# The relative bias of a second attention: from reversing products on TensorE to keys kept in reverse order

## The reference

```
rel = (kj[None, :] - pad_len) - qi[:, None]
bias = rel_bias[:, jnp.clip(rel, -REL_CLIP, REL_CLIP) + REL_CLIP]      # (8 heads, 257 numbers each)
s = jnp.einsum('bhqd,bhkd->bhqk', q_blk, kb).astype(jnp.float32) + bias
valid = (start - pad_len + kj) >= 0
p = jax.nn.softmax(jnp.where(valid, s, -jnp.inf), axis=-1)
return jnp.einsum('bhqk,bhkd->bhqd', p.astype(vb.dtype), vb)
```

## Time and profile before

| | us |
|---|---|
| median of 3 runs | 2052.92 (2052.65 to 2053.29) |
| the profiled execution: its own time | 2052.41 |
| the profiled execution: span | 2050.5 |
| PE busy | 1834.5 (89%) |
| DVE busy | 774.1 (38%) |
| ACT busy | 496.1 (24%) |
| POOL busy | 47.6 (2%) |

### The profile page before, as it was taken

One profiled execution on the slowest core, in us unless ns is written; L12 is line 12 of the kernel. 1 busy time (PEld: TensorE's weight loads), 2 busy tenths in 40 slices (PEclk: granted clock), 3 DMA queues, 4 the chain that ended last, 5 costly groups with the idle time before them and its releaser, 6 DMA issues. The chain is left out here.

```text
span 2050.5 us, 24148 instructions
## 1 busy us (share of the span) xinstructions
PE 1834.5 (89%) x9870; PEld 1133.4 (55%) x9871; DVE 774.1 (38%) x1035; ACT 496.1 (24%) x573; POOL 47.6 (2%) x74
## 2 busy tenths in 40 slices
PE   5989687999999988989898994898799989988998
PEld 5864464333333323333333231876699977568887
DVE  5535553112222112211221122548545466455444
ACT  3323411001010101010010001423334343334442
POOL 5000000000000000000000000100000000000000
PEclk9999898999999999999999997899899999989999
DMA  8549558999999999999999996534354544664551
GB/s 289 177 124 327 178 215 369 417 427 429 428 429 428 429 428 429 428 429 428 429 428 429 428 427 231 165 134 164 120 206 164 192 141 161 210 225 142 200 190 61
DMA packets 133235, 597.27 MB, mean 291 GB/s; under 512 B 16720, under 2 KB 16856, under 8 KB 108464
## 3 DMA queue, kind: packets, MB, share of 16 engines
q1 hardware_dynamic: 120096, 587.23, 72.4%
q10 hardware_dynamic: 12528, 7.50, 1.3%
q0 software_dynamic: 544, 1.59, 0.2%
HBM read 595.17 MB, written 1.11 MB: 291 GB/s over the span
## 5 line engine op out<-in xcount | busy, mean ns | idle before, releaser
L167 DVE TENSOR_TENSOR wl<-raw,wh 128x2048 fp32r<-128x2048 f32 x126 | 285.0, 2299 | 85.9 <-ACT wh L161 85.6
L161 ACT ACTIVATE wh<-raw 128x2048 fp32r<-128x2048 f32 x126 | 236.7, 1910 | 202.5 <-PE banks L195 120.2
L1200 PE MATMUL banks<-moe_halves,xs 128*64 128x512 f32 x1024 | 234.1, 605 | 12.0 <-DMA moe_halves<-in_w_exp_in 12.0
L211 PE MATMUL banks<-xth,wh 128*128 128x256 f32 x800 | 227.0, 284 | 7.0 <-DVE xtl L272 6.7
L211 PE MATMUL banks<-xtl,wh 128*128 128x256 f32 x800 | 225.8, 282 | 0.0
L211 PE MATMUL banks<-xth,wl 128*128 128x256 f32 x800 | 225.5, 282 | 0.0
L1249 DVE COPY hid<-banks 128x512 f32<-128x512 f32 x32 | 22.1, 691 | 521.5 <-PE banks L1200 521.5
L1200 PEld LDWEIGHTS banks<-moe_halves,xs 128*64 128x64 f32 x1024 | 71.0, 139 | 161.0 <-issue 128.8
L211 PEld LDWEIGHTS banks<-xth,wh 128*128 128x128 f32 x800 | 150.6, 188 | 8.1 <-DVE xtl L272 7.1
L211 PEld LDWEIGHTS banks<-xth,wl 128*128 128x128 f32 x800 | 152.0, 190 | 0.0
L211 PEld LDWEIGHTS banks<-xtl,wh 128*128 128x128 f32 x800 | 151.7, 190 | 0.3
(11 more groups left out here) (355 smaller groups left out, 2088.3 us busy)
## 6 DMA issues: line engine op xcount, KB each, us to landing
moe_halves<-in_w_exp_in SPq DMA_DIRECT2D x64, 2048.0 KB, 34.7
moe_left<-in_w_exp_in SPq DMA_DIRECT2D x34, 2048.0 KB, 33.5
moe_halves<-in_w_exp_out SPq DMA_DIRECT2D x32, 2048.0 KB, 31.1
raw<-in_mlp_w SPq DMA_DIRECT2D x64, 1024.0 KB, 5.7
raw<-in_w_exp_in SPq DMA_DIRECT2D x30, 2048.0 KB, 34.7
raw<-in_ada_w SPq DMA_DIRECT2D x48, 1024.0 KB, 5.8
raw<-in_w_exp_out SPq DMA_DIRECT2D x18, 2048.0 KB, 31.1
moe_left<-in_w_exp_out SPq DMA_DIRECT2D x14, 2048.0 KB, 33.9
```

What stands on the lines that cost most here:

```text
L161: act.activation(c.wh[:, slot], c.raw[:, slot], ACT.Copy).then_inc(c.high_ready, 1)
L167: dve.tensor_tensor(c.wl[:, slot], c.raw[:, slot], c.wh[:, slot].bitcast(F32), ALU.subtract).then_inc(c.low_ready, 1)
L211: mm = pe.matmul(out, w[:, slot, k, cols], x[:, k0 + k, :], start=first and k == 0 and j == 0 and b % 2 == 0, stop=last and k == CK - 1 an ...
L1200: mm = pe.matmul(c.bank[hid_banks(c, par) + pn][half * HALF:half * HALF + HALF, :], c.xs[:, 2 * k + r, own * CAP:own * CAP + CAP], st.slot ...
```

## The change

The keys of the second attention are stored in reverse order when DVE takes them out of PSUM (negative step in the output of L527, panel 4). Scores then have their keys reversed, and a bias with reversed keys is one that a skewed transfer can lay out directly. POOL reverses the 511 numbers of each head once (`rel_back`, one more copy), stores them, and reads them with 16 skewed transfers of 128x256 (a head and a half of the queries each) in the place of 8 of 128x384. It adds the mask, read in reverse, to each head's bias (8 additions of 128x512 at the end of its list), so that DVE's one addition per unit brings bias and mask. `c.flip` and the 16 products with it are gone, and PE's wait for the transfers with them; DVE waits for `bias_ready` at unit 8 instead. DVE writes the weights of the second attention with a negative step (L768), which puts the keys back in order before PE turns them; the values are untouched. Several small tiles move: the mask is local to phase_in, `rel_wide` lies in `c.at`, `cv` and `sig` in `c.stats`, and `c.acts` is made with the experts' other tiles.

```diff
-    c.rel = c.sb("rel", [P, HB, 384], ctx=ctx)
+    c.rel = c.sb("rel", [P, HB, TT, S], ctx=ctx)
...
-            pool.dma_start(rel_rows, rel_wide[:, :]).then_inc(rel_stored, 16)
+
+            done(pool.tensor_copy(rel_back[:, 0:511], rel_wide[:, 510::-1]))
+            pool.dma_start(rel_rows[:, 0:511], rel_back[:, 0:511]).then_inc(rel_stored, 16)
             pool.wait_ge(rel_stored, 16)
             for h in range(HB):
-                pool.dma_start(c.rel[:, h, :], bass.AP(tensor=rel_rows.tensor, offset=h * 512, ap=[[1, P], [1, 384]])
-                               ).then_inc(c.rel_loaded, 16)
-            done(pool.memset(c.flip[:, :], 0.0))
-            done(pool.affine_select(out=c.flip[:, :], in_=c.flip[:, :], compare_op=ALU.not_equal, fill=1.0,
-                                    base=1 - P, pattern=[[1, P]], channel_multiplier=1))
...
+                for m in range(TT):
+                    pool.dma_start(c.rel[:, h, m, :], bass.AP(tensor=rel_rows.tensor, offset=h * 512 + m * P,
+                                                              ap=[[1, P], [1, S]])).then_inc(c.rel_loaded, 16)
...
+            pool.sem_inc(c.bias_ready, 1)
+            pool.wait_ge(c.rel_loaded, 16 * HB * TT)
+            for h in range(HB):
+                done(pool.tensor_tensor(c.rel[:, h], c.rel[:, h], mask[:, :, ::-1], ALU.add))
             pool.sem_inc(c.bias_ready, 1)
...
-                        last = dve.tensor_scalar(outs[p][:, 2 * b:2 * b + 2, :],
+                        out = outs[p][:, 2 * b:2 * b + 2, ::-1] if p == 4 else outs[p][:, 2 * b:2 * b + 2, :]
+                        last = dve.tensor_scalar(out,
...
-                                   start=True, stop=u < diff)
-                    if u >= diff:
-                        mm = pe.matmul(out, c.flip[:, :], c.rel[:, 2 * h + j, P - m * P:P - m * P + S],
-                                       start=False, stop=True)
+                                   start=True, stop=True)
...
-                if u + 1 == diff:
-                    pe.wait_ge(c.rel_loaded, 16 * HB)
...
-                b = c.alibi[:, h, m] if u < diff else c.mask[:, m]
-                dve.tensor_tensor(s[:, u % 2], c.psum[:, 2 * (u % 2):2 * (u % 2) + 2, 0:S],
-                                  b.unsqueeze(1).to_broadcast([P, 2, S]), ALU.add).then_inc(biased, 1)
+                if u == diff:
+                    dve.wait_ge(c.bias_ready, 2)
+                b = (c.alibi[:, h, m].unsqueeze(1).to_broadcast([P, 2, S]) if u < diff
+                     else c.rel[:, 2 * h:2 * h + 2, m])
+                dve.tensor_tensor(s[:, u % 2], c.psum[:, 2 * (u % 2):2 * (u % 2) + 2, 0:S], b, ALU.add
+                                  ).then_inc(biased, 1)
...
-                    dve.tensor_tensor(a[:, u % 2], e[:, u % 2], share[:, :].unsqueeze(2).to_broadcast([P, 2, S]),
+                    dve.tensor_tensor(a[:, u % 2, :, ::-1], e[:, u % 2], share[:, :].unsqueeze(2).to_broadcast([P, 2, S]),
```

More of the change, by code:

```diff
@@ L71, in make_mixing @@
     c.vb = c.sb("vb", [P, TT, 512], ctx=ctx)
-    c.mask = c.sb("mask", [P, TT, S], ctx=ctx)
     c.alibi = c.sb("alibi", [P, HA, TT, S], ctx=ctx)
-    c.rel = c.sb("rel", [P, HB, 384], ctx=ctx)
+    c.rel = c.sb("rel", [P, HB, TT, S], ctx=ctx)
 def make_experts(c):
@@ L86, in make_experts @@
     c.back = c.sb("back", [P, S], ctx=c.moe)
+    c.acts = c.sb("acts", [P, KT, CAP], ctx=c.moe)
     make_routing(c)
@@ L400, in phase_in @@
     c.gates = c.sb("gates", [P, TT, 2 * D], ctx=c.mix)
-    c.flip = c.sb("flip", [P, P], ctx=c.mix)
     c.at = c.sb("at", [P, 2, 512], ctx=c.mix)
@@ L424, in phase_in @@
         shift = c.sb("ln_in_shift", [P, D], ctx=local)
-        rel_wide = c.sb("rel_wide", [HB, 512], ctx=local)
+        mask = c.sb("mask", [P, TT, S], ctx=local)
+        rel_wide = c.at[0:HB, 1, :]
+        rel_back = c.sb("rel_back", [HB, 512], ctx=local)
         dist = c.sb("dist", [P, TT, S], ctx=local)
@@ L464, in _ @@
             done(pool.tensor_copy(rel_wide[:, hi + 1:512], rel_wide[:, hi:hi + 1].to_broadcast([HB, 511 - hi])))
-            pool.dma_start(rel_rows, rel_wide[:, :]).then_inc(rel_stored, 16)
+            done(pool.tensor_copy(rel_back[:, 0:511], rel_wide[:, 510::-1]))
+            pool.dma_start(rel_rows[:, 0:511], rel_back[:, 0:511]).then_inc(rel_stored, 16)
             pool.wait_ge(rel_stored, 16)
             for h in range(HB):
-                pool.dma_start(c.rel[:, h, :], bass.AP(tensor=rel_rows.tensor, offset=h * 512, ap=[[1, P], [1, 384]])
-                               ).then_inc(c.rel_loaded, 16)
-            done(pool.memset(c.flip[:, :], 0.0))
-            done(pool.affine_select(out=c.flip[:, :], in_=c.flip[:, :], compare_op=ALU.not_equal, fill=1.0,
-                                    base=1 - P, pattern=[[1, P]], channel_multiplier=1))
-            done(pool.memset(c.mask[:, :, :], 0.0))
+                for m in range(TT):
+                    pool.dma_start(c.rel[:, h, m, :], bass.AP(tensor=rel_rows.tensor, offset=h * 512 + m * P,
+                                                              ap=[[1, P], [1, S]])).then_inc(c.rel_loaded, 16)
+            done(pool.memset(mask[:, :, :], 0.0))
             for m in range(TT):
-                done(pool.memset(c.mask[0:CHUNK, m, m * P + CHUNK:S], NEG))
+                done(pool.memset(mask[0:CHUNK, m, m * P + CHUNK:S], NEG))
                 if m < TT - 1:
-                    done(pool.memset(c.mask[CHUNK:P, m, m * P + P:S], NEG))
+                    done(pool.memset(mask[CHUNK:P, m, m * P + P:S], NEG))
             done(pool.iota(dist[:, :, :], pattern=[[P, TT], [-1, S]], base=0, channel_multiplier=1,
@@ L487, in _ @@
                 done(pool.tensor_scalar(away[:, :, :], dist[:, :, :], -2.0 ** (-8.0 * (h + 1) / HA), None, ALU.mult))
-                done(pool.tensor_tensor(c.alibi[:, h], away[:, :, :], c.mask[:, :, :], ALU.add))
+                done(pool.tensor_tensor(c.alibi[:, h], away[:, :, :], mask[:, :, :], ALU.add))
+            pool.sem_inc(c.bias_ready, 1)
+            pool.wait_ge(c.rel_loaded, 16 * HB * TT)
+            for h in range(HB):
+                done(pool.tensor_tensor(c.rel[:, h], c.rel[:, h], mask[:, :, ::-1], ALU.add))
             pool.sem_inc(c.bias_ready, 1)
@@ L597, in phase_attend @@
         ss = c.sb("ss", [P, TT, HA], ctx=local)
-        cv = c.sb("cv", [P, KT], ctx=local)
-        sig = c.sb("sig_c", [P, KT], ctx=local)
+        cv, sig = c.stats[:, 0].rearrange("p a b -> p (a b)")[:, 0:KT], c.stats[:, 1].rearrange("p a b -> p (a b)")[:, 0:KT]
         part = ModPart(c, 0, 0, FIRST_MOD, 7, at[0:FIRST_MOD, 0, :], a[:, 0].rearrange("p j s -> p (j s)"), "mod0a_")
@@ L1324, in phase_experts @@
     c.weighed = c.sb("weighed", [P, TT, SLOTS], ctx=c.exp)
-    c.acts = c.sb("acts", [P, KT, CAP], ctx=c.exp)
     c.gate_half = c.sb("gate_half", [P, 8, CAP], ctx=c.exp)
```

## The result

The changed kernel takes 2034.59 us (median of 4 runs, 2033.55 to 2036.45), the one before beside it 2052.83 us (4 runs, 2052.65 to 2053.29). The ratio is 0.9915, 95% interval 0.9903 to 0.9927: 18.2 us faster. The profiled execution took 2035.56 us with a span of 2033.7 us; against the 2050.5 us of before that is 16.8 us, and this is the difference between the two traces.

The account below looks back on a forecast made before the run. PE's list was taken to bound the second attention; 15.0 us saved less 0.8 lost in the first units gave 14.2 off 2052.41, 2038.2 us, plus 0.5 for the median: 2038.7 us, range 2036.8 to 2042.0.

Parts of the forecast that it names:

- What PE's removed products are worth: Second attention on PE: scores fall from 2.51 to 0.63 us a unit, 15.0 us over 8 units.
- Rival 1: Second attention: the score pair doesn't overlap, or only in part; 10.1 us saved, 2042.8 us; chance 0.08.
- The first units: First iterations of the second attention: DVE's 2.87 us cycle rules, losing 0.8 us, bounds 0 and 2.
- What the change adds: Reversed DVE writes, POOL's extra copy and additions, and 0.5 MB more skewed reads: taken to cost nothing.
- rivals 2 and 5: DVE's reversed writes are slower: twice the time, 2040.2 us, chance 0.07; many times slower, 2061 us, chance 0.03.
- rival 3: phase_in: POOL's eight additions hold DVE so that a panel comes late; 1.6 us, 2040.3 us; chance 0.04.
- Does the gain reach the end? All that follows hangs on PE: After the second attention: expert loads wait for PE, so the whole 14.2 us reaches the end.
- rival 4: Stages after the attention: gain given back by the experts' stream or TensorE's clock; if all, 2052.9 us; chance 0.03.

Follow-up runs that it names:

- b_pairs: Kernel before with each unit's two key products next to each other, the two reversing products behind them, nothing removed: 2044.69 us, ratio 0.9961.
- b_noflip: Kernel before without the 16 reversing products and nothing in their place, so the relative bias is left out: 2218.65 us, ratio 1.0816.
- a_wait65: Changed kernel with 130 more already met waits (65 real instructions) at the start of PE's list: 2038.31 us, ratio 0.9935.
- a_pad65: Changed kernel with 65 empty instructions early in PE's list, which never became part of the program: 2034.17 us, ratio 0.9911.
- b_pad191: Kernel before with 191 empty instructions early in PE's list, which never became part of the program: 2052.18 us, ratio 0.9999.

## Why the prediction came out as it did

**What PE's removed products are worth: right.** Predicted were 0.63 us for the pair, a period of 3.11 us, and 14.2 us off the second attention; measured are 0.63, 3.10 and 14.39. The term of 15.0 us was 10.1 for the products taken out and 5.0 for the pair running side by side; b_pairs, which keeps all four products, has the pair at 0.63 us and so shows the second part by itself, and b_noflip has the whole. Rival 1 falls. That 14.39 comes so close to 14.2 is in part luck: in two other traces with the same attention a late chunk makes it 13.65 and 13.19, inside the loss of 0 to 2 us that was allowed for.

**The first units: right.** Starts 2.88, 2.71, 2.72 and 3.12 us apart, with a DVE wait of 0.18 us, against a forecast of 2.87 for two iterations and then 2.7.

**What the change adds: right, nothing.** The reversed writes keep 0.69 and 1.29 us (rivals 2 and 5 fall), POOL ended at 68.9 us, where 68 to 81 was forecast, and PE got no wait in phase_in (rival 3 falls). The start of the additions was forecast too late, at about 57 us instead of 52.27: the steps ahead of them, 4.0 us behind at the mask (30.99 instead of 27.02), lost less time on the way this time and were 1.0 us behind at the end. The cost beside POOL's additions was 1.1 to 1.6 us per pair of low parts, where rival 3 had 5.3 and the cover was 4.50 us. One reading under this term was too wide: not every DVE operation over 512 numbers takes 0.68 to 0.69 us, since a TENSOR_SCALAR of 128x512 in the experts takes 0.43; it holds for the operations that the change touches. The Trainium skill's "SBUF — State Buffer", section "Who interferes with whom", told of this exclusion; with eight additions in a row the trace agrees (2.08 us each instead of 1.29), and no wait came of it.

**"Does the gain reach the end? All that follows hangs on PE": this step failed.** It took 14.2 us over to the end unchanged. Up to the last combining product that holds: 13.39 us there, which is 14.39 less the 0.92 of the late start and 0.1. But what follows hung on PE's sequencer at one place, where no row had been read. There the branch became 5.9 us shorter and the wait for `in_ln_b` 2.3 us longer, a net of 3.6 us that the sum had at nothing. 13.4 + 3.6 = 17.0, against 16.8 us between the spans. Of the 18.2 us between the medians the other 1.4 are spread: the profiled executions lie 1.0 us above (after) and 0.4 us below (before) their medians.

a_wait65 is the test of this account. It is the change with PE's list at its old length, which is what the prediction took it for without saying so. It takes 2038.31 us, 13.6 us less than the kernel before beside it; forecast were 2038.7 us and 14.2 us less. So the terms that were summed were sound, and the one missing is what the position of the code does to the branch.

**Given back later (rival 4)** happened in part only, 2.3 us, and not by the experts' stream, whose first load is issued 13.0 us earlier (270.05 instead of 283.05), as the prediction read from SP's waits, if not the full 14.

## What to carry to other kernels

Where two products on different partitions have a product over all partitions between them, put the two next to each other: the order alone was worth 6.5 us in this attention. An edit that changes the number of an engine's instructions can change a branch far behind it, by 5.9 us here, so follow a gain past every branch, and repeat the run with the list brought back to its old length by real instructions before a difference of this size is put down to the edit. And where a stall goes away, look at which small load stands behind big ones in the next block (some 5 us here).

## What the hardware did that I had not expected

- PE's taken branch over the skipped code costs 371 ns or 6.3 us, by nothing but the position of the list: 371 ns at shifts of -65 and +191 instructions, 6.3 us at 0, in all seven traces of the table (six kernels). Which positions are good between these was not tried.
- Two float32 products over all 128 partitions, into different banks, run in 1.06 us next to each other (b_pairs), but take 0.63 us each, 1.26 in all, where they alternate with products of 64 partitions. Where these 0.2 us come from is open.
- At the end of the attention PE's clock varies with the execution. The last two products at L662 and L336 took 1.97 and 1.92 us at half clock after, and L336 1.04 us before. It is not the change: of the same programs, a_pad65 had L336 at 1.05 us and b_pad191 at 1.92. The windows of 20 us, after and then before; the columns are the busy times of PE, PEld, DVE, ACT and POOL, the granted clock, DMA share and GB/s:

```profile
200.00:220.00 20.00, 10.67 (x62) 6.44 (x54) 14.91 (x24) 9.07 (x15) 0.00 (x0) 0.66 0.79 287
```

```profile
213.50:233.50 20.00, 8.44 (x62) 5.28 (x54) 14.36 (x22) 7.97 (x11) 0.00 (x0) 0.83 0.60 213
```

The clock was 0.66 and 0.83. The lead over the kernel before was 13.47 us at the last chunk of ada_w, 12.13 at the slow L336, and 13.0 again at the first load for the experts.
